# Ten weight buffers, four of them in the arena, for the second mixture of experts of a two-block kernel

## The reference

```python
def expert_choice_ffn(h, w_router, w_gate, w_up, w_down):
    B, S, D = h.shape
    cap = CAPACITY_FACTOR * S // N_EXPERTS_2
    aff = jax.nn.softmax((h @ w_router).astype(jnp.float32), axis=-1)
    gates, idx = lax.top_k(jnp.swapaxes(aff, 1, 2), cap)
    xe = jax.vmap(lambda hb, ib: hb[ib])(h, idx)
    hid = jax.nn.silu(jnp.einsum('becd,edf->becf', xe, w_gate)) * jnp.einsum('becd,edf->becf', xe, w_up)
    ye = jnp.einsum('becf,efd->becd', hid, w_down) * gates[..., None].astype(h.dtype)
    bidx = jnp.arange(B)[:, None, None]
    return jnp.zeros_like(h).at[bidx, idx].add(ye)
```

## Time and profile before

| | us |
|---|---|
| median of 3 runs | 1767.87 |
| profiled execution | 1774.85 |
| its span | 1773.0 |
| PE busy | 1430.0 (81%) |
| DVE / ACT / POOL busy | 432.1 / 294.7 / 123.0 |
| moved by DMA | 513.64 MB, mean 290 GB/s |
| chain that ended last | PE 60%, DMA 26%, DVE 5% |

### The profile page before, as it was taken

One profiled execution on the slowest core, in us unless ns is written; L12 is line 12 of the kernel. 1 busy time (PEld: TensorE's weight loads), 2 busy tenths in 40 slices (PEclk: granted clock), 3 DMA queues, 4 the chain that ended last, 5 costly groups with the idle time before them and its releaser, 6 DMA issues.

```text
span 1773.0 us, 25841 instructions
## 1 busy us (share of the span) xinstructions
PE 1430.0 (81%) x11063; PEld 831.9 (47%) x11063; DVE 432.1 (24%) x878; ACT 294.7 (17%) x656; POOL 123.0 (7%) x233
## 2 busy tenths in 40 slices
PE   5999999999988888888888499777876765856764
PEld 2856866768553434244324187577432321312321
DVE  2011235330362221222222535353410000000002
ACT  1101213540011111111111113332100100101000
POOL 4000022000000000000000004211000000000000
PEclk8999989999989989999999899877989898988987
DMA  9674362645446999999999651100559999999995
GB/s 350 155 290 167 111 238 102 228 178 191 166 167 290 427 429 428 428 429 428 428 429 428 262 208 27 64 4 26 218 220 430 427 429 429 428 429 428 429 428 216
DMA packets 87451, 513.64 MB, mean 290 GB/s; under 512 B 9913, under 2 KB 14298, under 8 KB 62802
## 3 DMA queue, kind: packets, MB, share of 16 engines
q1 hardware_dynamic: 83570, 503.49, 69.9%
q0 software_dynamic: 3808, 9.08, 2.2%
HBM read 507.66 MB, written 3.15 MB: 288 GB/s over the span
## 4 chain that ended last, share of the span: by engine, by line
PE 60%; DMA 26%; DVE 5%; issue 4%; ACT 3%; POOL 1%; SPq 1%; another core or an unknown queue 0%; POOLq 0%; DVEq 0%; ACTq 0%
PE ps L1248 48%; DMA ring<-in_w_e_up 17%; DMA ring<-in_exp_w 7%; PE ps L1679 4%; PE ps L1848 4%; DMA ring<-in_ada_w 1%; DVE arena L2514 1%; PE ps L1664 1%; ACT arena L1023 1%; PE ps L2117 1%; ACT arena L1013 1%; DMA arena<-in_causal 1%; PE ps L1292 0%; SPq L562 0%; DVE stats L2159 0%
## 5 line engine op out<-in xcount | busy, mean ns | idle before, releaser
L1248 PE MATMUL ps<-ring,arena 128*32 128x512 f32 (+4 forms) x3444 | 468.1, 655 | 182.5 <-DMA ring<-in_w_e_up 89.1
L1248 PEld LDWEIGHTS ps<-ring,arena 128*32 128x32 f32 (+1 forms) x3444 | 134.3, 125 | 460.2 <-issue 385.0
L1248 PE MATMUL ps<-hTs,ring 128*128 128x256 f32 (+2 forms) x1120 | 248.0, 383 | 4.1 <-DMA ring<-in_w_in 3.5
L1248 PEld LDWEIGHTS ps<-hTs,ring 128*128 128x128 f32 (+2 forms) x1120 | 211.5, 189 | 39.6 <-DMA ring<-in_w_in 3.9
L1679 PE MATMUL ps<-arena 128*128 128x512 f32 x256 | 117.5, 601 | 29.0 <-DVE arena L2514 29.0
L1248 PE MATMUL ps<-arena 128*128 (+5 forms) x576 | 135.8, 391 | 4.6 <-POOL arena L701 2.4
L1248 PEld LDWEIGHTS ps<-arena 128*128 128x128 f32 (+1 forms) x576 | 120.4, 288 | 18.9 <-issue 10.4
L1248 PE MATMUL ps<-ring,hTs 128*128 128x512 f32 (+2 forms) x288 | 101.8, 512 | 0.0
L1679 PEld LDWEIGHTS ps<-arena 128*128 128x128 f32 x256 | 46.0, 189 | 103.0 <-ACT arena L1025 57.1
L2805 DVE TENSOR_TENSOR arena<-arena,ps 64x512 f32<-64x512 f32 x16 | 11.0, 690 | 301.5 <-ACT arena L1208 301.5
L2514 DVE COPY arena<-ps 128x512 f32<-128x512 f32 x32 | 22.1, 692 | 251.5 <-PE ps L1248 251.5
(11 more groups left out here) (442 smaller groups left out, 1223.2 us busy)
## 6 DMA issues: line engine op xcount, KB each, us to landing
ring<-in_exp_w SPq DMA_DIRECT2D x96, 2048.0 KB, 18.6
ring<-in_w_e_gate SPq DMA_DIRECT2D x32, 2048.0 KB, 18.8
ring<-in_w_e_up SPq DMA_DIRECT2D x32, 2048.0 KB, 23.3
ring<-in_w_e_down SPq DMA_DIRECT2D x32, 2048.0 KB, 24.2
ring<-in_w_in SPq DMA_DIRECT2D x22, 2048.0 KB, 14.8
ring<-in_ada_w SPq DMA_DIRECT2D x12, 2048.0 KB, 16.4
ring<-in_w_out SPq DMA_DIRECT2D x4, 2048.0 KB, 11.6
ring<-in_w_br_hg SPq DMA_DIRECT2D x2, 2048.0 KB, 8.6
```

The costliest lines, as they stand in the source:

```text
L1248: return nc.tensor.matmul(o, lhsT, rhs, start=start, stop=stop)
```

## The change

The second mixture of experts no longer uses the ring's numbering. It has eight up buffers and two down buffers (`up_slots`, `down_slots`). Six of the ten are the ring's, four lie in the arena: one each at AR 8192 and AR 4096 for up tiles, and at AR 12288 and AR 16384 for the down tiles. Even experts use up buffers 0 to 3, odd ones 4 to 7; both use the same two down buffers. Semaphores are `up_loaded` (one for each pair of tiles) and `down_loaded`.

SP's list starts with all six tiles of expert 0 and the four up tiles of expert 1. Its loop then asks for the down tiles of the next expert first, each behind the `down2_tiles` of this one, and after them for the up tiles of the expert after the next.

What lay in those parts of the arena moves: scores, affinities, the choice, `XE` and `YE` to `hTs`; the hidden values to `vv`, where SiLU and product now share one buffer; the gates to `cst`; the zero row and half of the norm weights to `brow`, the other half to `colv`. The norm weights are loaded in two parts by POOL, the first right after the masks, and the last product is made in two halves. Several semaphores of other stages are merged into common names with higher counts (`route_step`, `squares_ready`), each wait still for the same event.

```diff
--- before.py
+++ after.py
@@ -396,7 +396,7 @@
         ones_row = ident[0:1, 0:1].to_broadcast([1, P])
         logitT = arena(4)[0:36, 0:256]
-        scoreT = arena(7)[0:NE2, 1024:1280]
+        scoreT = hTs[0:NE2, 0:256]
@@ -502,18 +502,26 @@
 
         xf = v3(arena(0), TT)
         onep, gatep = v3(arena(1)[:, 0:1024], TT), v3(arena(1)[:, 1024:2048], TT)
-        XE = v3(arena(2)[:, 0:1024], KC)
-        xeb = [v3(arena(4)[:, 1024 + 256 * i:1280 + 256 * i], KC) for i in range(2)]
+        XE = v3(hTs[:, 0:1024], KC)
         gateR = v4(arena(4)[:, 1536:1792], TT, 4)
-        sg2, hid2 = arena(5)[0:64, 0:512], arena(5)[0:64, 512:1024]
-        HT2 = arena(4)[:, 0:512]
-        YE = arena(5)[:, 1024:2048]
-        fg = arena(6)[:, 0:1024]
-        zrow = arena(6)[0:1, 1024:1536]
+        HT1 = arena(4)[:, 0:512]
+        HT2, hid2 = vv[:, 0:512], vv[0:64, 512:1024]
+        gateR2 = v4(cst[:, 128:384], TT, 4)
+        YE = hTs[:, 1024:2048]
+        fg = (colv[:, 0:512], brow[:, 1024:1536])
+        zrow = brow[0:1, 704:832]
+
+        up_at = [ring[:, (N2 + m) % RING * TILE:(N2 + m) % RING * TILE + TILE] for m in range(3)]
+        up_at += [AR[:, 8192:12288], AR[:, 4096:8192]]
+        up_at += [ring[:, (N2 + m) % RING * TILE:(N2 + m) % RING * TILE + TILE] for m in range(3, 6)]
+        up_slots = [v3(a, 4) for a in up_at]
+        down_slots = [v3(AR[:, o:o + TILE], 4) for o in (12288, 16384)]
+        up_loaded = [S(f"up{k}_loaded") for k in range(4)]
+        down_loaded = [S(f"down{k}_loaded") for k in range(2)]
         aff, rank = v3(st[:, 72:104], TT), v3(st[:, 202:234], TT)
         amax, asum = st[:, 104:106], st[:, 106:108]
-        affT, work, sel = (arena(7)[0:NE2, 256 * i:256 * i + 256] for i in range(3))
-        top8 = arena(7)[0:NE2, 768:776]
+        affT, work, sel = (hTs[0:NE2, 256 * i:256 * i + 256] for i in range(1, 4))
+        top8 = hTs[0:NE2, 1024:1032]
         mmax, msum = st[:, 166:174], st[:, 190:198]
         kark, c2rk = st[:, 174:177], st[:, 111:114]
 
@@ -605,34 +613,46 @@
             for n in range(R2, N2):
                 plain_tile(n)
 
-            def tile2(e, m, at):
-
-                name, half = (("w_e_gate_2", 0), ("w_e_up_2", 0), ("w_e_gate_2", 1), ("w_e_up_2", 1),
-                              ("w_e_down_2", 0), ("w_e_down_2", 1))[m]
-                src = pxk(A[name][e])[:, 4 * half:4 * half + 4, :]
-                if name == "w_e_down_2":
-                    src = pxk(A[name][e][half * 512:(half + 1) * 512, :])
-                sp.dma_start(slot(N2 + at, (4, 1024)), src).then_inc(loaded[(N2 + at) % RING], 16)
+            def up_tile(e, m, k):
+
+                src = pxk(A[("w_e_gate_2", "w_e_up_2")[m % 2]][e])[:, 4 * (m // 2):4 * (m // 2) + 4, :]
+                sp.dma_start(up_slots[k], src).then_inc(up_loaded[k // 2], 16)
+
+            def down_tile(e, m):
+
+                src = pxk(A["w_e_down_2"][e][m * 512:(m + 1) * 512, :])
+                sp.dma_start(down_slots[m], src).then_inc(down_loaded[m], 16)
 
             sp.wait_ge(S("cu_ready"), 1)
             for j in range(4):
                 for q in range(4):
                     sp.dma_start(lags[32 * j:32 * j + 32, q::4, :], CU[32 * q:32 * q + 32, :, j:j + 284])\
                         .then_inc(S("lags_loaded"), 16)
-            for m in range(6):
-                if m == 1:
-                    sp.wait_ge(S("y_done"), 1)
+            tile_read(sp, N2 - RING)
+            up_tile(0, 0, 0)
+            sp.wait_ge(S("y_done"), 1)
+            for m in range(1, 3):
                 tile_read(sp, N2 + m - RING)
-                tile2(0, m, m)
-            with sp.Fori(0, (NE2 - 1) // 3) as i:
-                for j in range(3):
-                    for m in range(6):
-
-                        if m < 4:
-                            sp.wait_ge(S("up2_tiles"), i * 6 + (2 * j + m // 2 + 1 + UP0))
-                        else:
-                            sp.wait_ge(S("down2_tiles"), i * 6 + (2 * j + m - 3))
-                        tile2(i * 3 + (j + 1), m, m)
+                up_tile(0, m, m)
+            up_tile(0, 3, 3)
+            for m in range(2):
+                down_tile(0, m)
+            sp.wait_ge(S("mix_ready"), 1)
+            up_tile(1, 0, 4)
+            for m in range(1, 4):
+                tile_read(sp, N2 + 2 + m - RING)
+                up_tile(1, m, 4 + m)
+            with sp.Fori(0, (NE2 - 2) // 2) as i:
+                for j in range(2):
+                    for m in range(2):
+                        sp.wait_ge(S("down2_tiles"), i * 4 + (2 * j + m + 1))
+                        down_tile(i * 2 + (j + 1), m)
+                    for m in range(4):
+                        sp.wait_ge(S("up2_tiles"), i * 4 + (2 * j + m // 2 + 1 + UP0))
+                        up_tile(i * 2 + (j + 2), m, 4 * j + m)
+            for m in range(2):
+                sp.wait_ge(S("down2_tiles"), 2 * (NE2 - 2) + m + 1)
+                down_tile(NE2 - 1, m)
             sp.wait_ge(S("out_ready"), 1)
             sp.dma_start(out.rearrange("(t p) d -> p t d", p=P), x).then_inc(S("stored"), 16)
             sp.wait_ge(S("stored"), 16)
@@ -743,6 +763,7 @@
             pool.wait_ge(S("down_done"), NE1)
             load(brow[:, 0:MSK_A.shape[1]], A["masks"], "masks_loaded")
+            load(fg[1], A["final_norm_g_2"][0, 512:1024].partition_broadcast(P), "fg_loaded")
             halves()
@@ -802,15 +823,15 @@
             halves()
-            pool.wait_ge(S("zeros2_ready"), 1)
-            load(fg, A["final_norm_g_2"][0].partition_broadcast(P), "fg_loaded")
+            all_out(pool, "h4T", 8)
+            load(fg[0], A["final_norm_g_2"][0, 0:512].partition_broadcast(P), "fg_loaded")
             pool.wait_ge(S("onehot_ready"), 2)
             with pool.Fori(0, NE2 // 4) as i:
                 for j in range(4):
 
                     pool.wait_ge(S("turned2"), i * 4 + (j + 1))
                     for t in range(TT):
-                        ins = nc.gpsimd.tensor_copy(gateR[:, t], mid(gatep[:, t, bass.ds(i * 128 + 32 * j, 32)], 4))
+                        ins = nc.gpsimd.tensor_copy(gateR2[:, t], mid(gatep[:, t, bass.ds(i * 128 + 32 * j, 32)], 4))
                     ins.then_inc(S("gate_ready"), 1)
             halves()
 
@@ -1205,7 +1226,7 @@
                     act.wait_ge(S("up2_tiles"), i * 8 + (2 * j + 2 + UP0))
-                    nc.scalar.activation(sg2, ps[0:64, (j % 2) * 512:(j % 2) * 512 + 512], ACT.Silu)\
+                    nc.scalar.activation(hid2, ps[0:64, (j % 2) * 512:(j % 2) * 512 + 512], ACT.Silu)\
                         .then_inc(S("silu2_ready"), 1)
                     act.wait_ge(S("turned2"), i * 4 + (j + 2))
@@ -2079,9 +2100,9 @@
                         wt = []
                         for g in range(2):
-                            n = N2 + 6 * m + 2 * half + g
-                            pe.wait_ge(loaded[n % RING], i * 64 + load_count(n))
-                            wt.append(slot(n, (4, 1024)))
+                            k = 4 * (m % 2) + 2 * half + g
+                            pe.wait_ge(up_loaded[k // 2], i * 64 + 32 * (m // 2 + 1))
+                            wt.append(up_slots[k])
...
@@ -2100,13 +2121,12 @@
                     pe.wait_ge(S("hidT_ready"), i * 4 + (m + 1))
                     for part in range(2):
-                        n = N2 + 6 * m + 4 + part
-                        pe.wait_ge(loaded[n % RING], i * 64 + load_count(n))
+                        pe.wait_ge(down_loaded[part], i * 64 + 16 * (m + 1))
                         for half in range(2):
                             for q in range(4):
                                 ins = mm(ps[32 * q:32 * q + 32, 1024 + 512 * half:1536 + 512 * half],
                                          HT2[:, 64 * q + 32 * part:64 * q + 32 * part + 32],
-                                         slot(n, (4, 1024))[:, q, half * 512:half * 512 + 512], part == 0, part == 1)
+                                         down_slots[part][:, q, half * 512:half * 512 + 512], part == 0, part == 1)
                         ins.then_inc(S("down2_tiles"), 1)
 
                     pe.wait_ge(S("ye0_ready"), i * 4 + (m + 1))
@@ -2802,7 +2822,7 @@
                 for j in range(4):
                     dve.wait_ge(S("silu2_ready"), i * 4 + (j + 1))
-                    tt(hid2, sg2, ps[64:128, (j % 2) * 512:(j % 2) * 512 + 512], ALU.mult).then_inc(S("hid2_ready"), 1)
+                    tt(hid2, hid2, ps[64:128, (j % 2) * 512:(j % 2) * 512 + 512], ALU.mult).then_inc(S("hid2_ready"), 1)
                     dve.wait_ge(S("down2_tiles"), i * 8 + (2 * j + 2))
@@ -2813,8 +2833,11 @@
             rms_norm(x, x, None)
-            dve.wait_ge(S("fg_loaded"), 16)
-            say(tt(x[:], x[:], mid(fg, TT), ALU.mult), "out_ready")
+            dve.wait_ge(S("fg_loaded"), 32)
+            for half in range(2):
+                c = slice(half * 512, half * 512 + 512)
```

(36 more changed lines are left out.)

10 lines of the change are left out of this document (5 added, 5 removed).

## The result

The changed kernel takes 1757.49 us (median of 6 runs, 1753.26 to 1759.11), the kernel before on the same chip 1767.49. The ratio is 0.9929, with a 95% interval from 0.9913 to 0.9945: 12.5 us less, between 9.7 and 15.4. The ratio is an estimate from all runs and not the quotient of the two medians, which differ by 10.0 us. Forecast were 11.1 us less and 1757.

A forecast was written before the change was run, and what follows sets the result against it. The second mixture was taken as bound by its weight stream (427 to 430 GB/s), not TensorE. Terms -19.6 + 8.4 + 0.1 gave -11.1 us, so 1757 us against the median of 1767.87; range 1749 to 1765.

The forecast's parts named there:

- Step 1: Before expert 0: ten tiles in instead of six, 86 remain instead of 90, 19.6 us less to stream.
- Step 2: SP's queue after the first ten tiles: restart waits for expert 0's first down products, 8.36 us later.
- rival D: Stream restart: all four tiles count and it comes no later, gain 18 to 19.6 us, 1749; chance 0.07.
- Step 3: Steady stream: PE frees the down buffer 10.2 to 11.3 us after u3 lands, with 29.4 us of tiles asked.
- rival C: SP stands too long at the down buffers and the stream runs dry; slower, up to 1786 us; chance 0.04.
- Step 4: PE's start: expert 1 loses its 4.31 us wait; u3 of expert 2 is in at 1346.8 against 1358.7.
- Step 5: Tail: transfer order unchanged; the last norm-weight multiply, split in two, adds 0.1 us.
- Step 6: Norm-weight load, moved buffers, renamed semaphores and added transfers beside the serial chain: taken to cost zero.
- Rival B: Stream parts drift apart in the longer queue: u3 up to 7.3 us late, gain 3.8, 1764; chance 0.12.

The follow-up runs named there:

- Eight ahead: The changed kernel with only two of expert 1's up tiles asked early, the other two behind expert 0's first up half: 1757.06 us, ratio 0.9934 to the kernel before.
- Six ahead: The changed kernel's buffers and edits, but expert 1's up tiles asked where the old kernel asked them: 1767.19 us, ratio 1.0005 to the kernel before.
- the change again: The changed kernel unaltered, run again as reference beside the variants: 1756.47 us, ratio 0.9942 to the kernel before.
- first turn: The changed kernel with two up tiles asked ahead of the down tiles in SP's first turn only: 1751.60 us; second run 1750.79 us.
- first and last: The changed kernel with two up tiles asked ahead of the down tiles in SP's first and last turns only: 1751.78 us; second run 1748.98 us.
- half first again: Second run of the changed kernel with two up tiles asked ahead of the down tiles in every turn: 1750.96 us, ratio 0.9903 to the kernel before.
- half first: The changed kernel with two up tiles asked ahead of the down tiles in every turn, first run: 1747.73 us, ratio 0.9884 to the kernel before.
- six ahead, late: The changed kernel with expert 1's four up tiles asked only behind expert 0's first down tile: 1778.20 us, ratio 1.0051 to the kernel before.
- the short queue: The changed kernel with up tiles of the expert after the next asked only when the next one's up halves are multiplied: 1761.90 us, ratio 0.9955 to the kernel before.

## Why the prediction was right, point by point

**Step 1, four tiles more in front.** Right. They were in before expert 0 began, and the stream behind the restart is 442.2 - 422.8 = 19.4 us shorter (forecast 19.6). Eight ahead gives 442.2 - 432.5 = 9.7 for two tiles. Six ahead gives none.

**Step 2, the late restart.** Right in kind and sized well. From the add the restart comes at 60.4 and 62.6 us against 54.1, so 6.3 and 8.5 later (forecast 8.4). These differences mix two things, the order of the queue and TensorE's clock, and the profiles can be sorted by the second. Here are 20 us of PE's gather (the 16 products that pick a group's tokens) and first products, at the same place behind the add, in the change again (0.65 granted; the change's row above has 0.79):

```profile
1281.00:1301.00 20.00, 15.88 (x80) 9.81 (x83) 5.39 (x11) 2.42 (x5) 0.52 (x2) 0.65 0.00 1
```

And here are expert 0's first products, first in the change, then in the change again:

```profile
1293.63 4.06 PE L1269 MATMUL ps<-ring,hTs 128*32 128x512 f32 x34 [1.42 <-ACT hTs L1224]
```

```profile
1295.01 5.66 PE L1269 MATMUL ps<-ring,hTs 128*32 128x512 f32 x34 [1.42 <-ACT hTs L1224]
```

From the start of these products to the restart ask it is 12.46 us in the one and 14.07 in the other. The early restarts fall into the same two kinds. In four profiles the granted clock was 1.00 over the first 3.6 us of these products, and the restart comes 3.69 to 3.85 us behind their start (eight ahead, first turn, first and last, half first again). In five it was 0.54 to 0.62, and the restart comes 5.21 to 5.50 us behind (before, six ahead, half first, and the second runs of first turn and of first and last). The price of the late restart itself can be read within one profile, where the clock is the same for both: in each variant with an early restart SP asks for the first down tile of expert 1 8.6 to 8.8 us behind the restart ask. I had 8.4, from the kernel before.

The rest is the clock, 2.2 us between the two profiles of the change, which rival D named. It moves the restart in every version, with the change or without. The profile of the change had the full clock there and that of the kernel before the low one (0.54), so 13.0 us lie behind the add and not 11. The profile of the change again had the low clock (0.55), and there it is 10.7. The forecast was thus right in its terms, but that 1757 met 1757.49 to half a microsecond is luck: the runs tell the gain only to some 3 us.

That the price is paid in full is shown by "six ahead, late" (9.0 us slower) and by "half first" (taking it out gives 17 to 20 us in all).

**Step 3, the stream stays full.** Right. DMA share is 1.01 from 1307 to 1728. PE frees the first down buffer of expert 2 at 1350.30, 10.7 us after u3 of expert 2 was in (1339.64; step 4), where the forecast had 10.2 to 11.3 and rival C needs 29.4.

**Step 4, PE at the start.** Right. Expert 1's second up half starts without a wait, and the first wait for a tile is that for u3 of expert 2. It starts at 1339.64, 33.5 us after the restart ask (forecast 32.1):

```profile
1339.64 1.07 PE L1269 MATMUL ps<-ring,hTs 128*32 128x512 f32 x2 [3.82 <-DMA arena<-in_w_e_up]
```

PE's own waits for the second mixture's tiles sum to 80.0 us (the three rows above) against 90.9 before: 10.9 less, forecast about 11.

**Step 5, the tail.** The two half products take 1225 and 1219 ns in place of 2292, and the store is asked 2.38 us after the first one starts, where it was 2.32: 0.06 us more, I had 0.1. The gap of 0.05 us that I took for VectorE does not stand in the rows that I named; its timeline before has 0.03 ahead of that product (1764.56 + 1.68 to 1766.27). The tail of the profile is 0.4 us longer, which is the last up half at 5.49 us instead of 5.15.

**Step 6, at nothing.** Right, by "six ahead". The added transfers do not slow the serial chain either: from the add to expert 0's first products it is 48.63 us before and 47.95 in the change, though DMA moves 279 GB/s there (1247 to 1293) where it moved 149 (1254 to 1300). In the change again, at the low clock of the profile of before, it is 48.56. POOL's second load took 0.54 us and ended 5.4 us ahead of its next work, as its timeline shows:

```profile
1008.43 0.54 POOL L664 DMA_DIRECT2D brow<-in_final_norm_g  x1
1014.40 0.56 POOL L701 TENSOR_TENSOR stats<-stats,cst 128x1 f32<-128x1 f32 x1 [5.42 <-DVE stats L2406]
```

**Rival B** was the rival I gave most to, because the queue would be up to ten tiles deep where it was about five. The runs show that the short queue and the long one leave the same 7.4 to 7.5 us between the last up half and the stream's end. **Rival D** had the right price and the wrong way to it. The gain of 17 to 20 us is there once the restart does not come later, but that did not take a PE that is 8 us sooner at the down tiles; it took another order in SP's queue. I took the late restart as given by the change. I did not see that two up buffers are free before it and that the queue's order alone keeps them empty.

## What to carry to other kernels

Where a stream of weights is the bound, as here, its end is (when it restarts) + (tiles still to come) x (time of one) + (tail). More buffers pay only by the tiles that land in otherwise idle time, less what the restart loses. In one in-order queue the first wait behind the pause decides that restart, so put in front of it the tile whose buffer comes free first: here that gave another 4.9 to 8.7 us for no buffer at all (from 1756.47 to 1751.60 with the first turn and to 1747.73 with every turn, on one chip), and the profiles put the late restart at 8.6 to 8.8. And compare profiles from an anchor just ahead of the changed stage, since two spans of single executions differed here by up to 10 us in front of it.

## What the runs showed of the hardware

From the restart to the stream's end a 2 MB tile cost between 4.913 and 4.926 us (442.2 / 90 and 423.6 / 86). It was the same with all tiles in the ring (before, 4.913) as with four of ten buffers in the arena (six ahead, 4.913), and the short queue, with four to six tiles asked, has the highest of these figures. Not expected was the spread ahead of the stage: the same add between 1242.92 and 1252.56 us in thirteen profiles. Its cause stays open.
